# Sixteen more bytes per slot in the weight ring buffers of a two-block transformer kernel

## What is computed

```python
# first block
h = layer_norm(ALPHA*x + 0.5*swiglu(x, gate, up, down))          # D_FF = 2816
mix = concat(hgrn2(h @ w_in ...), spatial_gating(h @ w_in ...)) @ w_out
h = layer_norm(ALPHA*h + mix)
h = layer_norm(ALPHA*h + cross_attention(h, mem, wq, wk, wv, wo))  # 256 memory rows
h = layer_norm(ALPHA*h + 0.5*swiglu(h, gate2, up2, down2))
# second block
x = h + concat(attention(rmsnorm(h) @ w_in_2), pool(...)) @ w_out_2
x = x + swiglu(rmsnorm(x), w_gate_2, w_up_2, w_down_2)
```

## Time and profile before

| | us |
|---|---|
| median of 3 runs | 1688.51 (1688.37 to 1689.0) |
| span of the profiled execution | 1686.8 |
| TensorE busy in it | 1668.9 |
| GpSimd busy | 697.5 |
| VectorE busy | 644.4 |
| ScalarE busy | 597.0 |
| mean share of the DMA queue with the weights | 32.0% |

### The profile page before, as it was taken

How to read it: one execution, slowest core, us unless ns; L and a number is a source line. 1 busy time by engine, 2 the same in 40 slices (tenths; PEclk the granted TensorE clock), 3 DMA queues, 4 the chain that set the end, 5 groups by cost and what they waited for, 6 DMA issues and landing times.

```text
span 1686.8 us, 20746 instructions
## 1 busy us (share of the span) xinstructions
PE 1668.9 (99%) x8353; PEld 1397.9 (83%) x8353; DVE 644.4 (38%) x1067; ACT 597.0 (35%) x911; POOL 697.5 (41%) x385
## 2 busy tenths in 40 slices
PE   9999999999999999999999999999999999999998
PEld 7888888899888888899888888888768988888887
DVE  4111111267665776656111211276763512121122
ACT  4222222247445464436222122256573422122220
POOL 4453444446563353025443444433321544344432
PEclk9999999999999999999999999999999999999999
DMA  7333233333221454123333243332112333324322
GB/s 206 91 98 100 76 112 100 88 117 104 66 76 51 126 155 131 38 75 99 91 99 100 69 119 100 90 117 63 44 32 57 106 100 98 90 81 119 93 82 76
DMA packets 296521, 157.58 MB, mean 93 GB/s; under 512 B 5233, under 2 KB 293098, under 8 KB 296426
## 3 DMA queue, kind: packets, MB, share of 16 engines
q1 hardware_dynamic: 296426, 156.26, 32.0%
HBM read 154.14 MB, written 2.10 MB: 93 GB/s over the span
## 4 chain that ended last, share of the span: by engine, by line
PE 92%; ACT 3%; DVE 3%; issue 1%; POOL 0%; DMA 0%; SPq 0%; DVEq 0%; ACTq 0%
PE bank L480 22%; PE bank L481 22%; PE bank L484 22%; PE bank L2234 2%; PE bank L2231 2%; PE bank L2230 2%; PE bank L523 2%; PE bank L524 2%; PE bank L528 2%; PE bank L2673 2%; PE bank L509 1%; PE bank L503 1%; PE bank L504 1%; PE bank L2661 1%; PE bank L2421 1%
## 5 line engine op out<-in xcount | busy, mean ns | idle before, releaser
L410 POOL TENSOR_TENSOR wlo<-wraw,whi 128x1024 fp32r<-128x1024 f32 (+1 forms) x252 | 595.4, 2376 | 827.6 <-ACT whi L405 827.6
L480 PE MATMUL bank<-ahi,whi 128*128 128x512 f32 x1294 | 508.1, 393 | 0.0
L481 PE MATMUL bank<-alo,whi 128*128 128x512 f32 x1294 | 504.0, 389 | 0.0
L405 ACT CAST whi<-wraw 128x1024 fp32r<-128x1024 f32 (+1 forms) x284 | 284.6, 1026 | 240.3 <-PE bank L484 154.6
L484 PE MATMUL bank<-ahi,wlo 128*128 128x512 f32 x1294 | 321.1, 389 | 0.0
L480 PEld LDWEIGHTS bank<-ahi,whi 128*128 128x128 f32 x1294 | 243.0, 188 | 51.5 <-issue 1.4
L481 PEld LDWEIGHTS bank<-alo,whi 128*128 128x128 f32 x1294 | 243.0, 188 | 51.5 <-issue 1.4
L484 PEld LDWEIGHTS bank<-ahi,wlo 128*128 128x128 f32 x1294 | 242.9, 188 | 50.6
L1543 DVE SCALAR_TENSOR_TENSOR hval<-gate,bank 128x512 f32<-128x512 f32 x66 | 45.4, 687 | 553.0 <-PE bank L484 541.9
L959 ACT ACTIVATE gate<-bank 128x512 f32<-128x512 f32 x66 | 39.6, 600 | 507.6 <-PE bank L484 500.1
L1552 DVE SCALAR_TENSOR_TENSOR res<-res,bank 128x512 f32<-128x512 f32 x80 | 54.1, 686 | 254.6 <-PE bank L484 181.2
(11 more groups left out here) (341 smaller groups left out, 2201.1 us busy)
## 6 DMA issues: line engine op xcount, KB each, us to landing
wraw<-in_ffn_w_gate SPq DMA_DIRECT2D x43, 512.0 KB, 3.7
wraw<-in_ffn_w_up SPq DMA_DIRECT2D x43, 512.0 KB, 3.7
wraw<-in_w_in SPq DMA_DIRECT2D x34, 512.0 KB, 3.8
wraw<-in_ffn_w_down SPq DMA_DIRECT2D x32, 512.0 KB, 3.6
wraw<-in_w_gate SPq DMA_DIRECT2D x22, 512.0 KB, 3.7
wraw<-in_w_up SPq DMA_DIRECT2D x22, 512.0 KB, 3.8
wraw<-in_w_out SPq DMA_DIRECT2D x16, 512.0 KB, 4.0
wraw<-in_w_down SPq DMA_DIRECT2D x16, 512.0 KB, 3.6
```

Of the source, the lines that this page charges most:

```text
L405: eng.copy(whi[:, b % 4, 0:n], wraw[:, b % RAW, 0:n]).then_inc(hi_ready, 1)
L410: eng.tensor_tensor(wlo[:, b % RAW, 0:n], wraw[:, b % RAW, 0:n], whi[:, b % 4, 0:n], ALU.subtract).then_inc(LO[b][0], 1)
L480: eng.matmul(o, w, xhi[:, k, :], start=(k == 0), stop=False)
L481: eng.matmul(o, w, xlo[:, k, :], start=False, stop=False)
```

## The change

Each slot of `wraw`, `wlo` and `whi` becomes 4 float32 (16 bytes) longer. The bytes at the end of a slot are never used. All instructions stay; the addresses of the slots move, and with them those of every tile allocated after `wraw`.

```diff
         alo = sb("alo", [P, KD, T], F32R)
-        wraw = sb("wraw", [P, RAW, KD * P])
-        wlo = sb("wlo", [P, RAW, KD * P], F32R, at=top[0] - RAW * KD * P * 4)
-        whi = sb("whi", [P, 4, KD * P], F32R)
+        SLOT = KD * P + 4
+        wraw = sb("wraw", [P, RAW, SLOT])
+        wlo = sb("wlo", [P, RAW, SLOT], F32R, at=top[0] - RAW * SLOT * 4)
+        whi = sb("whi", [P, 4, SLOT], F32R)
         mats = sb("mats", [P, C_N, P])
```

## The result

The changed kernel takes 1714.16 us (median of 4 runs, 1713.88 to 1714.75) against 1688.44 us: 1.0152 times the time before, 95% interval 1.0139 to 1.0166. The forecast was 1694.1 us, slower by 5.6; it is slower by 25.7.

A forecast was written before the change was run, and what follows sets the result against it. The prediction took TensorE's matmul count times spacing as the bound. Its terms, 7.0-0.5-1.9+1.0 = +5.6 us, added to the median 1688.5 gave 1694.1 us, with a range of 1677 to 1711.

The forecast's parts named there:

- The bound: Whole kernel: TensorE busy 1668.9 of 1686.8 us, so time is the number of matmuls times their spacing.
- Residues matter: TensorE matmuls: spacing depends on the start residues of weight and stream tiles; evidence called thin.
- rival of no dependence: Matmul spacing does not hang on start residue; nothing changes, 1688.5 us; chance 0.27.
- The period of 128 bytes: Weight slots against ahi: residues count modulo 128, so one of six wlo and one of four whi slots stay even.
- The price of an uneven pair: 512 columns on ahi/alo: 3192 matmuls whose start residues differ cost 2.2 ns more each, +7.0 us.
- the nearest row: Profile row of hid streaming over the same weights, 228.9 ns, taken as the spacing for shifted ahi/alo pairs.
- The rival in which every shifted pair costs 233 ns: 512 columns on ahi/alo and hid: shifted pairs behave like mv, +32 us, 1720; chance 0.07.
- Hid: 512 columns on hid: a quarter of 928 whi matmuls becomes even and gains 2.2 ns each, -0.5 us.
- 256 columns: 256 columns on ahi/alo: 896 matmuls become uneven and get 2.1 ns less each, -1.9 us; mk and mv left.
- Re-settling: ahi blocks becoming even again: up to 0.05 us each, bounds nothing and 2.1 us, middle +1.0 us taken.
- Loads, cast and subtraction: Work on shifted slots stays hidden behind matmuls; rival of slower loads: under 4 us at the start, 1692, chance 0.03.

The follow-up runs named there:

- the sweep: Separate kernel, other engines idle: 48 float32r matmuls per sequence on resident tiles, one weight-to-stream start offset each; 226.8 ns at offset 0, 233.3 at 64 (512 columns).
- low slots alone: Kernel before with only wraw/wlo slots 16 bytes longer, filler keeping whi and arena residues modulo 256: 1697.92 us, 1.0054.
- the kernel with untouched loads and raw slots: Kernel before with only whi slots 16 bytes longer, filler keeping mats and arena residues modulo 256: 1700.49 us, 1.0069.
- both sweeps: The single-offset sequences plus a second set varying second-stream residue, weight pitch, continuation offset and width, other engines idle; none below 226.7 ns in the second at 512 columns.

## Why the prediction was wrong, point by point

**The bound: right.** The time is matmuls times spacing. Waits and other engines stayed as they were, the clock too but for 1.4 us in the profiled execution, and the time came out of start distances alone.

**Residues matter: right.** The rival of no dependence falls: with all other engines idle, the start of the weights against the stream moves the spacing between 226.6 and 234.3 ns. The rule of the Trainium skill that stood beside it (SBUF — State Buffer, Who interferes with whom) speaks of waiting on others, and it does not fall with the rival: offset 0 gives 226.7 ns and offset 32 233.3 ns whether the other engines are idle (the single sequences) or at work (the kernels), which agrees with it. What was wrong was to take two independent read ports as a sign that starts don't matter. No run here shows the ports.

**The period of 128 bytes: wrong.** I derived which slots stay even modulo 128 and got slot 2 of whi at 226.7 ns. It stands at 232.7; its offset is 128, and the period is 256. No high slot stayed even. The trace before offered offsets 0 and 192 and, with the memory stationary, 64, so it could not settle the period, and the prediction did not say so. It had one hint: 192 (hid) and 64 (weights over mhi) are equal modulo 128 and stood at 228.9 and 233 ns, though in different layouts.

**The price of an uneven pair: the step that failed most.** I took hid's 2.2 ns for all pairs, as "the nearest row". The low and high matmuls on ahi/alo pay 5.3 ns on average, +21.9 us instead of +7.0. By the period of 256, 3876 of the 4104 are uneven, not 3192, and they pay 5.65 ns on average instead of 2.2: of the 14.9 us that the sum lacks here, 11.0 are the price and 3.9 the count. Hid in that layout at offset 192 is one of the cheapest uneven pairs. An ordinary uneven pair costs 6.6 ns (nearly all offsets in the sweep are at 232 to 234). The row for streaming weights, 233 ns, which I used as the upper bound, was the typical price; its pair lies at offset 64, where the sweep has 233.3. Bounds were right and the choice between them was not. The rival in which every shifted pair costs 233 ns (+32 us) had a chance of 0.07 and came nearest to the 25.7 us; the upper end of my range, 1711, was cut two thirds of the way to it.

**Hid: wrong sign.** I had -0.5 us, as a quarter of its pairs would become even. None did, and the cheap 192 was given up for others: +4.7 us.

**256 columns: right on ahi/alo, mk left out.** -1.9 us expected for ahi/alo, measured -1.6 once the stretch at half the clock is left out, so this term is nearly right. What the sum lacks is +0.8 for mhi/mlo, which I left out (mk has 192 matmuls, not 144), and +0.3 for hid. At 256 columns offset 0 is one of the worst and 64 the best of the sweep, but offsets 112, 144, 160 and 240 are as bad as 0.

**Re-settling: smaller for each block than I had it.** With slots that don't fit there is little left to settle into, and the change's trace does not give the term by itself. Where the run can settle (low slots alone), it costs 0.5 ns on 2736 high matmuls, 1.4 us over about 108 blocks that lose the run, 0.013 us each instead of up to 0.05. What I had not seen is its other side: a settled run survives an offset of 16, which is why block 7 (offset 144 and 16) runs at 226.7 after block 6's low half at offset 0.

**Loads, cast and subtraction: right.** TensorE's waits on the subtraction are 1.4 us against 1.3 before, and the kernel with untouched loads and raw slots loses 11.8 us all the same. The rule of the Trainium skill that warm matmuls start N/2.4 GHz plus about 2.5 ns apart (TensorE: Matmul & The Clock Gate, Wait — 56ns, not 53.3ns?) is met by no sequence here, where each matmul has a weight load of its own: 226.6 ns is the lowest steady value in the kernels and in both sweeps with 512 columns of float32r, 13.3 ns above the 213.3 of streaming and not 2.5.

What stays open is the mechanism behind the table: why 256 bytes, why there are two steady spacings at 256 columns, why offsets 0 and 64 in turn are as good as 0 alone, and why hid's layout is cheap at 192.

## What to carry to other kernels

When TensorE is busy all the time and waits for nothing, take the start-to-start distance of its matmuls by tile pair. If two pairs of one shape differ, compare where their tiles start before anything else. Keep ring slots at a pitch that is a multiple of 256 bytes and put stationary and streaming tiles at the same residue modulo 256 for 512 columns of float32r; padding slots to "spread" them cost 1.5% here, one misplaced filler of 32 bytes 1.7%. A price for a layout that the trace doesn't show should be measured in a sequence of single offsets, which takes one run; reading it from the nearest row took the cheapest case for the typical one.

## What the runs showed of the hardware

- The distance between float32r matmuls depends on the start of the weight tile minus the start of the stream tile, modulo 256 bytes (256 repeats 0, 384 repeats 128): 226.6 ns at 0, 228.3 at 240, 230.0 at 176, 232 to 234.3 at the other multiples of 16 (512 columns, two streams at one residue).
- At 256 columns the order is another: 113.3 ns at offset 64, 120.0 at 0, 116.7 to 120.3 elsewhere. At 448 columns offset 64 has 202.1 ns against 206.7 at 0. The best offset depends on the width.
- The spacing has a memory. At the start of a sequence at offset 0, and where the stream goes from hid back to ahi, between one and eleven matmuls, mostly at 224 to 236 ns, pass before 226.7 is reached; once settled it survives offsets of 16, 144 and 240 but not 4, 8, 32, 48, 128 or 224; and with 256 columns both 117.8 and 113.3 are steady, at offset 64 as at 192.
